# Grouped-query mixer in one block with its heads prepared beside the projection, attention by head pairs, zero products and earlier sums at the seams

## What is computed

```python
def odd_mixer(x, w_in, gqa_q_norm, gqa_k_norm, cos_c, sin_c):
    b, s, _ = x.shape
    g = GQA_HEADS // GQA_KV_HEADS                      # 16 // 4
    q, k, v = _split(x @ w_in, ODD_SPLITS)             # 1024, 256, 256 columns
    q = rms_norm(q.reshape(b, s, GQA_HEADS, GQA_HEAD_DIM), gqa_q_norm)      # head dim 64
    k = rms_norm(k.reshape(b, s, GQA_KV_HEADS, GQA_HEAD_DIM), gqa_k_norm)
    v = v.reshape(b, s, GQA_KV_HEADS, GQA_HEAD_DIM)
    q = apply_rope(q, cos_c[:, None, :], sin_c[:, None, :]).reshape(b, s, GQA_KV_HEADS, g, GQA_HEAD_DIM)
    k = apply_rope(k, cos_c[:, None, :], sin_c[:, None, :])
    ...   # softmax(q k^T / 8) v per head
```

## Time and profile before

| | |
|---|---|
| median of 3 runs | 2532.39 us (2532.22 to 2537.24) |
| the profiled execution | 2534.98 us, its span 2533.1 us |
| instructions | 30629 |
| PE, DVE, ACT busy | 2100.3, 1036.0, 709.0 us |
| mean granted clock | 0.906 |
| read from HBM | 621.76 MB, 246 GB/s over the span |

### The profile page before, as it was taken

How to read it: one execution, slowest core, us unless ns; L and a number is a source line. 1 busy time by engine, 2 the same in 40 slices (tenths; PEclk the granted TensorE clock), 3 DMA queues, 4 the chain that set the end, 5 groups by cost and what they waited for, 6 DMA issues and landing times. The chain is left out here.

```text
span 2533.1 us, 30629 instructions
## 1 busy us (share of the span) xinstructions
PE 2100.3 (83%) x12310; PEld 1408.4 (56%) x12316; DVE 1036.0 (41%) x1514; ACT 709.0 (28%) x987; POOL 72.6 (3%) x148
## 2 busy tenths in 40 slices
PE   7778867776767797777776899888999999888998
PEld 6466322222245562222222688775887888766886
DVE  3345100000045540000001676665776676665775
ACT  3523100100023430000010343434433343434332
POOL 0000000000001000000000000010000000010000
PEclk9868999899887899888988899987999999988999
DMA  9113999999980249999999655431565456431651
GB/s 332 43 43 120 393 426 427 426 426 427 426 332 34 96 186 427 425 426 427 427 427 410 209 190 194 156 125 50 183 199 166 156 177 231 131 103 52 198 182 42
DMA packets 192680, 623.69 MB, mean 246 GB/s; under 512 B 17543, under 2 KB 114921, under 8 KB 159849
## 3 DMA queue, kind: packets, MB, share of 16 engines
q1 hardware_dynamic: 192616, 622.84, 63.9%
HBM read 621.76 MB, written 1.05 MB: 246 GB/s over the span
## 5 line engine op out<-in xcount | busy, mean ns | idle before, releaser
L1752 PE MATMUL psum<-weight_ring,arena 128*32 128x256 f32 x4096 | 291.9, 440 | 148.9 <-DMA weight_ring<-in_w 148.4
L2022 PE MATMUL psum<-x_both,up_hi 128*128 128x512 f32 x1408 | 359.5, 397 | 0.8 <-DVE x_both L441 0.7
L1752 PEld LDWEIGHTS psum<-weight_ring,arena 128*32 128x32 f32 x4096 | 135.7, 123 | 307.8 <-DMA weight_ring<-in_w 192.1
L1769 PE MATMUL psum<-weight_ring,arena 128*32 128x512 f32 x1024 | 248.3, 651 | 54.3 <-DMA weight_ring<-in_w 49.1
L2022 PEld LDWEIGHTS psum<-x_both,up_hi 128*128 128x128 f32 x1408 | 258.0, 188 | 59.0 <-DVE x_both L441 4.4
L1802 DVE TENSOR_TENSOR arena<-arena,psum 128x256 f32<-128x256 f32 x32 | 13.5, 421 | 547.4 <-PE psum L1752 547.4
L547 PE MATMUL psum<-w_hi,x_both 128*128 128x512 f32 (+2 forms) x800 | 212.0, 394 | 17.8 <-DVE mix_lo L686 12.9
L2070 DVE TENSOR_TENSOR up_lo<-weight_ring,up_hi 128x2048 fp32r<-128x2048 f32 x88 | 201.3, 2292 | 19.4 <-ACT up_hi L2044 19.2
L2025 PEld LDWEIGHTS psum<-x_both,up_lo 128*128 128x128 f32 x1408 | 192.2, 188 | 15.6
L2025 PE MATMUL psum<-x_both,up_lo 128*128 128x256 f32 x1408 | 197.1, 282 | 0.0
L2082 DVE TENSOR_REDUCE arena<-psum 128x256 f32<-128x512 f32 x176 | 113.3, 686 | 187.1 <-PE psum L2025 187.1
(11 more groups left out here) (300 smaller groups left out, 2341.2 us busy)
## 6 DMA issues: line engine op xcount, KB each, us to landing
weight_ring<-in_w SPq DMA_DIRECT2D x192, 2048.0 KB, 25.7
weight_ring<-in_ffn_wg SPq DMA_DIRECT2D x44, 1024.0 KB, 5.5
weight_ring<-in_ffn_wu SPq DMA_DIRECT2D x44, 1024.0 KB, 8.0
weight_ring<-in_ffn_wd SPq DMA_DIRECT2D x44, 1024.0 KB, 5.0
weight_ring<-in_w_in SPq DMA_DIRECT2D x12, 2048.0 KB, 8.0
weight_ring<-in_w_o SPq DMA_DIRECT2D x4, 2048.0 KB, 19.7
weight_ring<-in_ple_gate_w SPq DMA_DIRECT2D x4, 2048.0 KB, 14.7
weight_ring<-in_w_out SPq DMA_DIRECT2D x4, 2048.0 KB, 8.0
```

The source lines that it names most:

```text
L1752: last = pe.matmul(ps[j * CAP:(j + 1) * CAP, 4 + k // 2, 0:QW], tokens_now[:, cc, :], w[:, c, j * QW:(j + 1) * QW], start=cc == 0, stop=cc ...
L1769: last = pe.matmul(ps[j * CAP:(j + 1) * CAP, 6 + h, :], hc[:, i, j * CAP:(j + 1) * CAP], w[:, jj, i, h, :], start=i == 0, stop=i == 1)
L2022: last = pe.matmul(ps[:, 4 + 2 * f + h, :], w_part[:, f, h, c, :], x_both[:, :, c, :], start=c == 0, stop=False, skip_group_check=True)
```

## The change

1. **Odd mixer.** The unit of keys and values is projected first (`matrix(..., 2 * KV_HEADS * HD)`). The norm weights are multiplied into the rotation's tables once (`gain_tables`, eight products of 64 elements a row, at k=0 and behind a wait for the parameters). Keys are rotated and scaled at k=5; queries 0 to 7 are rotated by DVE at k=5; queries 8 to 15 by POOL during the attention (`rotate_last`). The queries' root is not multiplied in: it is the `scale` of the exponential and a factor of the maximum (`row_scale`). No block ends between projection, attention and output product.
2. **Attention by pairs.** Score products of heads 2j and 2j+1 alternate, and so do their value products; copies to `mix_cols` go to DVE where nothing is masked.
3. **Zero products.** `idle_products(pe, n)` issues n products of zeros (128x512, bf16) into bank 7 ahead of waits at the seams.
4. **Sums at seams.** A semaphore after tile 0's last product lets DVE add tile 0 while TensorE does tile 1; the LayerNorm's offset goes from two POOL instructions to one on DVE.
5. **Output product of the odd mixer.** `part_mix(dve, 0)`, the split of half of its input, runs inside the attention at step 13, and ACT casts its first weights at the attention's end.

```diff
@@ plan_weights
-            matrix(t["w_in_odd"][0], ODD_IN)
+            matrix(t["w_in_odd"][0], ODD_IN, 2 * KV_HEADS * HD)
@@ column_steps
+    def idle_products(pe, n):
+        for _ in range(n):
+            pe.matmul(ps[:, SPARE_BANK, :], zeros_bf[:, 0:P], zeros_bf[:, :], start=True, stop=True)
         def turn(pe):
+            if rows_ready is None and roots_ready is None:
+                pe.wait_ge(zeros_made.sem, 1)
+            idle_products(pe, idle[0])
             setup_ready(pe)
...
             for a in range(TILES):
+                if a == TILES - 1:
+                    idle_products(pe, idle[1])
                 if rows_ready is not None:
                     rows_ready(pe, a)
...
+            idle_products(pe, idle[2])
@@ layer_norm_steps, layer_norm_root
-        dve.wait_ge(wanted.sem, wanted.at(1))
         dve.wait_ge(got.sem, got.at(1))
+        dve.scalar_tensor_tensor(out=stats[:, :, 15:16], in0=stats[:, :, 12:13], scalar=-1.0, in1=stats[:, :, 14:15],
+                                 op0=ALU.mult, op1=ALU.mult).then_inc(offset.sem, 1)
...
-        pool_chain.link(pool, pool.tensor_tensor(stats[:, :, 15:16], root, stats[:, :, 12:13], ALU.mult))
-        pool.tensor_scalar(stats[:, :, 15:16], stats[:, :, 15:16], -1.0, None, ALU.mult).then_inc(got.sem, 1)
@@ attention, TensorE
+            def score(j):
+                if 2 * j >= deep:
+                    pe.wait_ge(expd.sem, expd.at(TILES * (2 * j + 2 - deep)))
+                for a in range(TILES):
+                    for h in (2 * j, 2 * j + 1):
+                        last = pe.matmul(ps[:, bank(h), a * SEQ:a * SEQ + keys(a)], q_of(h)[:, a * P:(a + 1) * P],
+                                         k_of(h)[:, 0:keys(a)], start=True, stop=True)
+                last.then_inc(scores.sem, 2)
...
+            on_tensor(pe, -1)
+            for j in range(pairs + 2):
+                if j < pairs:
+                    score(j)
+                    on_tensor(pe, j)
+                if j >= 2:
+                    sum_values(j - 2)          # both heads, alternating
+                if 1 <= j < pairs + 1:
+                    turn(2 * j - 2), turn(2 * j - 1)
@@ attention, VectorE
+                if not masked and i >= 6 and i % 2 == 0:
+                    store(i // 2 - 3)
+            if not masked:
+                store(pairs - 2), store(pairs - 1)
@@ odd_mixer
-        to_columns(block, x, x_hi, x_lo, lambda act: None, load, rows_ready=tile_ready)
+        to_columns(block, x, x_hi, x_lo, lambda act: None, load, rows_ready=tile_ready, idle=(34, 6, 0))
+        def gain_tables(dve):
+            params_ready(dve)
+            for which in range(2):
+                for i in range(4):
+                    last = dve.tensor_tensor(rope_gained[...], rope_gqa[...], gain..., ALU.mult)
+            last.then_inc(tables_gained.sem, 1)
+        def finish_keys(dve):
+            dve_chain.link(dve, rotate_heads(dve, 0))
+            dve.wait_ge(rooted.sem, rooted.at(1))
+            for a in range(TILES):
+                last = dve.tensor_tensor(k_twice[:, a], heads_of(0)[:, a]..., root[:, a]..., ALU.mult)
+            last.then_inc(doubled.sem, 1)
         def heads_on_vector(dve, k):
+            if k == 0:
+                gain_tables(dve)
             if k == 1:
                 tables.reduce_angles(dve)
             if k == 4:
                 sum_heads(dve, 0)
             if k == 5:
-                params_ready(dve)
+                finish_keys(dve)
+                rotate_heads(dve, 1).then_inc(rotated.sem, 1)
                 sum_heads(dve, 1)
-                rotate_heads(dve, 0)
-                rotate_heads(dve, 1)
+        class Queries:                          # beside the attention
+            tensor, step -1:  wait doubled; 8 transposes of keys; wait rotated(1); 8 of queries; wait placed(2)
+            tensor, step 3:   wait rotated(2) and turned_kept(4); 8 transposes of queries 8 to 15; wait placed(4)
+            scalar, step -1:  2 copies of keys, 2 of queries, square_last;   step 5: 2 copies of queries
+            vector, step -1:  wait rooted(2);   step 1: sum_heads(dve, 2);   step 7: wait rooted(3)
+            vector, step 13:  wait stored(4); part_mix(dve, 0)
+            gpsimd:           rotate_last (6 products of 512 elements a row), root_heads(pool, 2)
@@ mix_out_norm, mix_out
+                    if (h, a) == (1, 0):
+                        dve.wait_ge(first_tile.sem, first_tile.at(1))
+                    else:
+                        job.wait(dve, h)
@@ ffn
-            dve.wait_ge(down_done.sem, down_done.at(steps_total))
             for a in range(TILES):
+                if a == 0:
+                    dve.wait_ge(first_tile.sem, first_tile.at(1))
+                else:
+                    dve.wait_ge(down_done.sem, down_done.at(steps_total))
@@ calls
+        to_columns(..., idle=(10, 0, 12))      # even projection, the kernel's start
+                   cast_first=True, idle=(26, 6, 8))     # both experts stages
+    rms_columns(..., 20)                       # both second mixers, and one ffn
+    ffn(..., 50)                               # after the second experts stage
+    ffn(..., 16)                               # twice, after mix_out
```

More of the change, by code:

```diff
@@ L550, in products @@
                                                  stop=cc == DC - 1 and w_part is low)
+                        if self.tile_done is not None and (i, half, a) == (self.units - 1, 1, 0) and w_part is low:
+                            last.then_inc(self.tile_done.sem, 1)
                 last.then_inc(self.done.sem, 1)
@@ new lines, in peaks @@
+                        last = dve.tensor_tensor(e_buf[:, h % deep, a, a * P:(a + 1) * P],
+                                                 src[:, a, a * P:(a + 1) * P], causal, ALU.add)
+                    dve_chain.link(dve, last)
+                    for a in range(TILES):
+                        last = dve.tensor_reduce(small[:, h % deep, a, 0:1], e_buf[:, h % deep, a, 0:keys(a)], AX,
+                                                 ALU.max)
+                else:
+                    last = dve.tensor_reduce(small[:, h % deep, :, 0:1], src, AX, ALU.max)
@@ L881, in attention, with normalise @@
-            if beside:
-                @block.gpsimd
-                def _(pool):
-                    beside.gpsimd(pool)
+                else:
+                    dve.scalar_tensor_tensor(out=small[:, h % deep, :, 1:2], in0=small[:, h % deep, :, 0:1],
+                                             scalar=-1.0, in1=row_scale(h), op0=ALU.mult,
+                                             op1=ALU.mult).then_inc(peak.sem, 1)
+            def normalise(h):
+                dve.wait_ge(expd.sem, expd.at(TILES * (h + 1)))
+                dve_chain.link(dve, dve.reciprocal(small[:, h % deep, :, 3:4], small[:, h % deep, :, 2:3]))
+                for a in range(TILES):
+                    last = dve.tensor_scalar(e_buf[:, h % deep, a, 0:keys(a)], e_buf[:, h % deep, a, 0:keys(a)],
+                                             small[:, h % deep, a, 3:4], None, ALU.mult)
+                last.then_inc(norm.sem, 1)
@@ new lines, in store @@
+            def store(j):
+                dve.wait_ge(summed.sem, summed.at(2 * j + 2))
+                dve.tensor_copy(mix_cols[:, mix_head // 2 + j, :], ps[:, 6 + j % 2, 0:SEQ]
+                                ).then_inc(stored.sem, 1)
+            on_vector(dve, -1)
+            for i in range(heads + 1):
+                if i < heads:
+                    peaks(i)
+                on_vector(dve, i)
+                if i >= 1:
+                    normalise(i - 1)
+                if not masked and i >= 6 and i % 2 == 0:
+                    store(i // 2 - 3)
@@ L885, in attention, with _ @@
+        if beside:
+            @block.gpsimd
+            def _(pool):
+                beside.gpsimd(pool)
         for s in (scores, norm, turned, kept, summed, peak):
@@ L887, in attention @@
         expd.advance(TILES * heads)
-        stored.advance(heads // 2)
+        stored.advance(pairs)
     def even_projection(block):
@@ new lines, in turn_queries, with place_queries @@
+        def turn_queries(pe, chunks, bank):
+            for i, c in enumerate(chunks):
+                for a in range(TILES):
+                    last = pe.transpose(ps[:, bank, i * SEQ + a * P:i * SEQ + (a + 1) * P],
+                                        h[:, a, c * P:(c + 1) * P], ident[:, :])
+            last.then_inc(turned.sem, 1)
+        def place_queries(act, chunk, bank, nth):
+            act.wait_ge(turned.sem, turned.at(nth))
+            act.copy(q_cols[:, chunk:chunk + 2, :], ps[:, bank, :].rearrange("p (c q) -> p c q", c=2)
+                     ).then_inc(placed.sem, 1)
```

543 lines of the change are left out of this document (295 added, 248 removed).

## The result

The changed kernel takes 2494.78 us (median of 4 runs, 2489.32 to 2496.19) where the kernel before takes 2534.53 (4 runs): a ratio of 0.9839, interval 0.9819 to 0.9859, 40 us faster. The forecast was 2478 in a range of 2462 to 2506: right in sign and inside the range, 17 us too low. The profiled execution's span is 2494.0 us, 39.1 less than before's.

What follows compares the result with a forecast made beforehand. Experts' stages were taken as bound by the DMA queue, the feed-forward by TensorE, with serial engine-to-engine chains between, which alone change. Savings summed to 54.6 us: 2480.4 for the profiled execution, 2478 for the median, range 2462 to 2506.

Steps and rivals of the forecast that it cites:

- the price of `gain_tables` at k=0: Odd projection: VectorE waits for parameters ahead of the low parts, TensorE stalls longer; cost 4.5 us, from 0 to 6.
- the first output product: Odd mixer: its output product starts at 825.5 instead of 844.43, 19 us earlier.
- both norms' seams behind mix_out: RMSNorm after mix_out, twice: diagonal products at full clock and the first tile's sum ahead, 3.5 us each, 7.0.
- R4: Rival: zero products themselves run at half clock and real products wait behind them; 12 us slower, 2547; chance 0.06.
- the odd output product's 1.6: Odd mixer's output product: its products start warm, 1.6 us more saved.
- the pair's pace: Odd mixer's attention: two heads take 3.65 us instead of 5.3, bound by VectorE; eight pairs save 13.2.
- At full clock near 0.12: 2.4 saved: RMSNorm's seams: 32 diagonal products, 0.19 each before, run near 0.12 behind zeros, saving 2.4 us.
- the start: Kernel's start: 16 products in 6.62 us become 16 x 0.23 = 3.7; 2.3 us saved, from -1 to 3.
- the first feed-forward: Norm between experts and feed-forward: 2.5 us and 0.45 of POOL, 3.0 saved.
- Other attentions ... 1.5 each: Latent attention 1.5 us in all (0 to 4); causal attention, twice, 1.5 each from value products (0 to 6).
- Some 21 us of the sum are clock, 12 norms and sums: Split of the 54.6 us saved: some 21 clock, 21 the odd mixer, 12 norms and sums.
- The router seams' clock: LayerNorm before both experts stages: 24 router products at full clock save 2.5 us, the second tile's transposes 0.4.

Runs made afterwards that it cites:

- k: Kernel before, with only the reduced angles on VectorE moved to half unit 3 and the sines on ScalarE to 4: 2525.23 us, ratio 0.9959.
- d: Changed kernel with single heads in the latent and causal attentions, pairs kept in the grouped-query one: 2490.95 us, ratio 0.9832.
- f: Changed kernel with the rotation of queries 8 to 15 on VectorE before its first maximum instead of on GpSimd: 2491.90 us, ratio 0.9834.
- h: Changed kernel with parameters' jobs at half unit 3, single heads in the causal attentions and more zero products at three places: 2473.84 us, ratio 0.9763.
- i: Changed kernel with one product of zeros over all array rows between the two heads' scores of each pair: 2499.51 us, ratio 0.9862.
- l: Changed kernel with twice as many zero products at every seam: 2527.98 us, ratio 0.9968.
- g: Changed kernel with more zero products at the start, the first feed-forward and ahead of the causal stretches' transposes: 2488.87 us, ratio 0.9825.
- b: Changed kernel with gained tables and reduced angles moved on VectorE to half unit 3, sines on ScalarE to 4: 2480.35 us, ratio 0.9785.
- e: Changed kernel with one head's products before the other's within each pair, scores and values, in all attentions: 2490.43 us, ratio 0.983.
- j: Kernel h with the norm's gains fetched through ScalarE's queue instead of SyncE's: 2469.24 us, ratio 0.9744.
- a: Changed kernel without its zero products: 2505.75 us, ratio 0.9889.
- c: Changed kernel with the grouped-query attention's products in the old order, one head after the other: 2501.44 us, ratio 0.9866.

## Why the prediction was right in sign and 17 us low

- **Right, with their sizes:** the chains add up (the stage lengths sum to the span's difference); the price of `gain_tables` at k=0 (4.5, measured 4.7); the first maximum (forecast 5.9 us behind the projection's end, measured 5.7); the first output product, by the odd mixer alone (19 earlier, measured 17.6); both norms' seams behind mix_out (7.0, 7.1); the end (1.2). R4 did not come: zeros ran at 0.22, all but the kernel's first ten, and stopped short of the waits. (R4's 2547 is counted from the profiled execution, the other cases from the median; from there it is 2545.)
- **Right by luck:** the odd output product's 1.6 (1.5 measured), since k reaches the same 22.6 us without the change and d, f, h, i and l, with it, do not.
- **Right in the sum, wrong in the reason, the pair's pace.** I took VectorE as the bound at 3.65 us a pair. Its work is 3.34, the pace is 3.93, and a loop through three engines sets it; i shows that the scores' length sits in it. I also read TensorE's work before as 2 x 2.2 us a pair, where it was busy all of 2 x 2.65; the 3.2 after came true (3.17). Up to the first maximum the forecast has 15.4 behind the projection's end (21.3 before, 5.9 after) and 15.6 came. From there to the output product it has 50.4 less 42.3, so 8.1, and 6.7 came: pairs gave 9.3 (13.2 before bubbles in the forecast), and the work moved into the attention took 2.5 of it. The sum of both, 23.5, missed by 1.2.
- **The first failed step: "At full clock near 0.12: 2.4 saved" applied to every seam.** It missed at the start (2.3 forecast, 0.2 measured) and at the first feed-forward (3.0, 0.1), 5 us together. At both I counted the zeros against the idle time, found that they fit, and did not ask what the remainder does: it was 2.8 us, and with it the clock fell in ten of fourteen cases, where over 1.4 us or less it held in every kernel. At the start that draw is the whole miss. At the first feed-forward it is not: g, b and e had the full clock there and gained nothing, since the gains' DMA, issued behind the ring's and landing 9 us later, was next in line. I did not look for what would be late next, and j shows that it was this DMA.
- **The second: "Other attentions ... 1.5 each".** The pairs' overlap of products was priced as a gain, and the causal attention shows none: ten stretches are 0.6 us longer than before, four 3.9. The profiled execution drew one of these four, so that the two terms are 7.5 us of the 15.5 that the sum had too much; the larger part of it is the clock's draw, and what pairs cost there stays open.
- **Mis-sized: the split of a seam between clock and sums.** "Some 21 us of the sum are clock, 12 norms and sums": a measures 11 for the zeros in the whole time and 12.0 in seven seams. I took 6.26 us of one seam as the diagonal products' length; without zeros they took 5.2 to 6.7 us in a. The router seams' clock, 2.9 each in the forecast, measured 1.8 and 1.4 (and 4.4 there is 4.25 when added up). With POOL's shorter chain, the sums ahead are worth 1.4 at a LayerNorm (1.35 forecast) and 1.9 behind mix_out (0.95 forecast).
- **What I did not see as a chance:** that before already lost 8.5 us at the parameters' wait. It stood in the earlier trace rows as 10.95 us of idle VectorE and 5.68 of TensorE. I priced the change's effect on it and not the wait itself.

## What to carry to other kernels

Filler products at a wait pay about 1.7 us a seam here, if they reach to the wait's end: with 2.8 us left idle behind them the clock fell in most executions, and one too many costs 0.22. Before pricing a shorter step, look for the next releaser in line behind it, above all for small DMAs that their queue issues late because large ones stand ahead; and put a wait for such a DMA as late in an engine's program as its result allows, since that one edit was worth more than a third of the whole change. When two heads fit the array's halves, either order of their products will do as long as nothing stands between them; the pace is then set by the loop through the other engines.

## What the runs showed of the hardware

- Products that use different row halves overlap without alternation: 8 in 1.13 us alternating and 1.14 one head after the other, 2.3 us once a product over all rows stands between the fours.
- With TensorE idle for 2.8 us behind the zeros the granted clock fell to 0.50 in ten of fourteen cases and held in four; over 0.3 to 1.4 us it held in each of the ten kernels with these counts of zeros. In the latent output product it rose at about 173.4 us in both kernels though the products began at 169.8 and 168.3, so of the 1.4 us gained ahead of it 0.7 were lost in it (24.2 to 24.9 us).
- The same code in the causal stretch (the changed kernel, b, c and f) took 79.0 to 79.2 us in four cases and 82.5 to 82.6 in four, the long ones with the clock at 0.50 for 44 us on end. A claim of 2 us there needs several profiles.
- A VectorE scaling of 128x256 beside GpSimd products took 2.66 us for two, 0.64 without.
- The gains' DMA took 8.9 us from issue to landing through SyncE's queue and 9.0 through ScalarE's at the same seam. Its earlier issue made the seam shorter, not its queue.
